# Two-level seven-product multiplication in the feed-forward up projections

## What is computed

```python
def swiglu(h, w_in, w_out):
    gt, up = jnp.split(h @ w_in, 2, axis=-1)
    return (jax.nn.silu(gt) * up) @ w_out
```

## Time and profile before

| | us |
|---|---|
| median of 3 runs | 3933.7 |
| the runs | 3933.52 to 3936.74 |
| span of the profiled execution | 3933.3 |

### The profile page before, as it was taken

One profiled execution on the slowest core, in us unless ns is written; L12 is line 12 of the kernel. 1 busy time (PEld: TensorE's weight loads), 2 busy tenths in 40 slices (PEclk: granted clock), 3 DMA queues, 4 the chain that ended last, 5 costly groups with the idle time before them and its releaser, 6 DMA issues.

```text
span 3933.3 us, 48502 instructions
## 1 busy us (share of the span) xinstructions
PE 3827.1 (97%) x18602; PEld 2867.3 (73%) x18602; DVE 2221.4 (56%) x3856; ACT 741.8 (19%) x1402; POOL 716.2 (18%) x570
## 2 busy tenths in 40 slices
PE   7999988999999999999999999999999999999998
PEld 3455567665555555688888877888789998778886
DVE  4255677354445313326564755654888888556546
ACT  2144455211110013421100000000311111100002
POOL 0048844000000000000000002120244343121200
PEclk9999999999999999999999999999999999999999
DMA  5244400222121121122322322232222222122321
GB/s 193 88 169 150 139 2 2 86 84 56 55 62 59 48 75 43 33 65 79 91 74 89 95 77 86 85 102 86 77 73 72 69 69 64 54 86 85 102 86 65
DMA packets 381407, 312.13 MB, mean 79 GB/s; under 512 B 9552, under 2 KB 349904, under 8 KB 381136
## 3 DMA queue, kind: packets, MB, share of 16 engines
q1 hardware_dynamic: 381264, 310.16, 25.3%
HBM read 308.03 MB, written 2.10 MB: 79 GB/s over the span
## 4 chain that ended last, share of the span: by engine, by line
PE 87%; POOL 5%; DVE 3%; ACT 2%; issue 1%; DMA 1%; POOLq 0%; SPq 0%; DVEq 0%; ACTq 0%
PE ps_lin L967 18%; PE ps_lin L867 10%; PE ps_d L967 9%; PE ps_lin L1741 6%; PE ps_d L867 5%; PE ps_c L967 4%; PE ps_lin L750 4%; PE ps_lin L767 3%; PE ps_d L750 3%; PE ps_lin L813 3%; PE ps_lin L1158 3%; PE ps_c L867 3%; POOL arena L3507 2%; PE ps_d L1530 2%; POOL arena L3504 2%; PE ps_c L750 2%
## 5 line engine op out<-in xcount | busy, mean ns | idle before, releaser
L3476 POOL TENSOR_TENSOR rstd<-square 128x512 f32<-128x512 f32 (+2 forms) x12 | 15.1, 1260 | 1542.5 <-ACT square L1919 1542.5
L967 PE MATMUL ps_lin<-arena,ring 128*128 128x256 f32 (+1 forms) x800 | 217.2, 424 | 1.1 <-DVE arena L2598 1.1
L867 PE MATMUL ps_lin<-arena,ring 128*128 128x256 f32 (+1 forms) x864 | 214.1, 401 | 0.0
L967 PEld LDWEIGHTS ps_lin<-arena,ring 128*128 128x128 f32 x800 | 151.8, 190 | 60.9 <-issue 2.9
L867 PEld LDWEIGHTS ps_lin<-arena,ring 128*128 128x128 f32 x864 | 164.2, 190 | 41.1
L967 PE MATMUL ps_lin<-hid_in,arena 128*128 128x256 f32 x832 | 188.6, 380 | 3.6 <-DVE arena L2625 3.6
L3479 POOL TENSOR_TENSOR rstd<-rstd,square 128x512 f32<-128x512 f32 (+2 forms) x58 | 75.5, 1301 | 630.9 <-ACT square L1919 630.0
L967 PE MATMUL ps_lin<-hid_in,mixed 128*128 128x384 f32 (+1 forms) x672 | 187.7, 432 | 0.0
L967 PE MATMUL ps_d<-arena,mixed 128*128 128x384 f32 (+1 forms) x672 | 187.7, 432 | 0.0
L2622 DVE TENSOR_TENSOR arena<-ring 128x1024 f32<-128x1024 f32 x84 | 102.9, 1225 | 146.3 <-PE ps_d L867 135.9
L967 PEld LDWEIGHTS ps_lin<-hid_in,arena 128*128 128x128 f32 x832 | 157.7, 190 | 27.7 <-DVE arena L2625 5.6
(11 more groups left out here) (546 smaller groups left out, 8101.4 us busy)
## 6 DMA issues: line engine op xcount, KB each, us to landing
ring<-in_ffn_w_in SPq DMA_DIRECT2D x88, 512.0 KB, 4.8
resid<-in_ada_w SPq DMA_DIRECT2D x20, 2048.0 KB, 7.9
ring<-in_mlp_w_up SPq DMA_DIRECT2D x64, 512.0 KB, 4.5
ring<-in_mlp_w_down SPq DMA_DIRECT2D x64, 512.0 KB, 4.4
ring<-in_attn_w_qkv SPq DMA_DIRECT2D x64, 512.0 KB, 4.8
ring<-in_ffn_w_out SPq DMA_DIRECT2D x32, 512.0 KB, 4.4
ring<-in_even_w_in SPq DMA_DIRECT2D x28, 512.0 KB, 5.0
ring<-in_sc_w_in SPq DMA_DIRECT2D x24, 512.0 KB, 4.6
```

Source lines behind the costliest of these rows:

```text
L867: last = mm(prod[i - 1], lhs[:, j, :], rhs(p), start=(g == j == 0), stop=(g == G - 1 and j == np_ - 1))
L967: last = mm(out, lhs[:, j, :], rhs[:, j, :], start=(j == 0), stop=(j == 3))
```

## The change

Both up projections work in 11 rounds of 256 gate and 256 up columns. The outer level cuts rows of the contraction in halves (H tiles 0 to 3 and 4 to 7), columns in gate and up, and tokens in halves, and has seven outer products in the order 1, 2, 7, 4, 5, 6, 3. Each outer product has 512 rows of contraction, 256 columns and half the tokens. It is done whole (two tiles, "a" and "b", of four matmuls of half the tokens) or is split once more in seven products of two matmuls of a quarter of the tokens: 192 columns in up0, 128 in up1. Outer product 4 is always whole, and in the first round only 1 and 2 are split: 62 of 77 are. The scheme is one in which the sums build on each other: inside a split product 1, 6, 7 and 4 accumulate in the same PSUM bank, and ScalarE copies its state out after 1, 6 and 7 ("partial") and 4 ("last_block"); 3 accumulates on 5.

GpSimd makes the four outer weight sums of a round (`outer_sums`), 1024 elements each, in the places of the loaded blocks. VectorE makes the four inner weight sums of a split product (`halves`, 256 elements each), the three blocks that are sums (`block_of`: "11", "22" and "12", a quarter of the tokens each, out of PSUM and a partial), the eight outer sums of a round (`outer_adds`, two tiles of half the tokens each), the products with the gate, and the inner sums of the inputs (`inner_inputs`, four each for six input blocks) and the outer ones T1 to T4. Partials and held products lie where constants were and in the norm's places. A round's four loads of 512 KB are issued as their places come free. Some semaphores are shared between loads. Product 3 of a split one and 4 come in TensorE's program after the next one's first products.

The diff's core:

```diff
+TWO_WIDTH, ROUNDS, OUTER = {"up0": T, "up1": LAT}, KF // 2, (1, 2, 7, 4, 5, 6, 3)
+OUTERS = 7 * ROUNDS
+INNER_SUMS = (1, 3, 2, 4)
+def outer(n):
+    return OUTER[n % 7]
+def split(n):
+    return 0 <= n < OUTERS and outer(n) != 4 and (n >= 7 or outer(n) < 3)
...
+SPLIT_LATER = {5: "T3", 6: "T1", 7: "T2", 8: "B22"}
+BLOCK_OF = {1: "B11", 2: "B21", 3: "B22", 4: "T4", 5: "T1", 6: "T2", 7: "T3"}
...
+    m["RAW2"] = {(1, 1): cut(ring, 0, 4, 2 * P), (1, 2): cut(ring, 1024, 4, 2 * P),
+                 (2, 1): cut(ring, 2048, 4, 2 * P), (2, 2): cut(ring, 3072, 4, 2 * P)}
+    m["SUM2"] = cut(big, 18944, 4, 2 * P)
+    m["OUT2"] = {1: m["RAW2"][1, 1], 2: m["RAW2"][1, 2], 3: m["RAW2"][2, 2], 4: m["RAW2"][2, 2],
+                 5: m["RAW2"][2, 1], 6: m["SUM2"], 7: m["SUM2"]}
...
+                for r in (1, 2):
+                    half_done(prev)(r - 1)
+                    for c in (1, 2):
+                        fill(0, r, c)
+                for i in range(1, ROUNDS):
+                    n = 7 * (i - 1)
+                    sp.wait_ge(s.two_sums, 4 * two_round(st, n) + 3)
+                    fill(i, 1, 1)
+                    if split(n + 4):
+                        sp.wait_ge(s.two_added, ADDED[st, n + 4, "half", 4])
+                    sp.wait_ge(s.two_made, MADE[st, n + 4, 4 if split(n + 4) else "b"])
+                    fill(i, 2, 1)
+                    sp.wait_ge(s.two_sums, 4 * two_round(st, n) + 4)
+                    fill(i, 1, 2)
+                    if split(n + 6):
+                        sp.wait_ge(s.two_added, ADDED[st, n + 6, "half", 4])
+                    sp.wait_ge(s.two_made, MADE[st, n + 6, 4 if split(n + 6) else "b"])
+                    fill(i, 2, 2)
...
+                def whole(n, t):
+                    b, w = mats[BLOCK_OF[outer(n)]], m["OUT2"][outer(n)]
+                    out = m["BANK2"][n % 2]["ab".index(t)][:, 0:hw]
+                    if t == "a":
+                        weights_there(n)
+                        if n < 7 and outer(n) == 3:
+                            pe.wait_ge(s.h_new, H_COUNT[late])
+                        elif n < 7:
+                            pe.wait_ge(s.two_added, ADDED[st, BLOCK_OF[outer(n)], 0])
+                        pe.wait_ge(s.two_taken, TAKEN[st, n - 2, 4 if split(n - 2) else "a"])
+                    elif split(n - 2):
+                        pe.wait_ge(s.two_added, ADDED[st, n - 2, 11])
+                    else:
+                        pe.wait_ge(s.two_taken, TAKEN[st, n - 2, "b"])
...
+                    c = slice("ab".index(t) * P, "ab".index(t) * P + P)
+                    steps(out, [(w[:, j, c], b[:, j, :]) for j in range(4)]).then_inc(s.two_made, 1)
...
+                def seventh(n, j):
+                    b, t = quarters(mats[BLOCK_OF[outer(n)]]), inner[BLOCK_OF[outer(n)]]
+                    w, ws = quarters(m["OUT2"][outer(n)]), m["HALF2"][n % 2]
+                    lhs, rhs = {1: (w[0], b[0]), 2: (w[2], b[2]), 3: (ws[4], b[3]), 4: (w[3], t[4]), 5: (ws[1], t[1]),
+                                6: (ws[2], t[2]), 7: (ws[3], t[3])}[j]
+                    chain_, second, fifth = m["BANK2"][n % 2]
+                    out = (second if j == 2 else fifth if j in (5, 3) else chain_)[:, 0:q]
+                    early = BLOCK_OF[outer(n)]
+                    if j == 1:
+                        weights_there(n)
+                        if n < 2:
+                            pe.wait_ge(s.h_new, H_COUNT[of] - KD + 4 * n + 2)
+                        else:
+                            pe.wait_ge(s.two_taken, TAKEN[st, n - 2, 4 if split(n - 2) else "a"])
+                    if j == 2:
+                        if n < 2:
+                            pe.wait_ge(s.h_new, H_COUNT[of] - KD + 4 * n + 4)
+                        elif split(n - 2):
+                            pe.wait_ge(s.two_added, ADDED[st, n - 2, 11])
+                        else:
+                            pe.wait_ge(s.two_taken, TAKEN[st, n - 2, "b"])
+                    if j == 5:
+                        pe.wait_ge(s.two_added, ADDED[st, n, "half", 1])
+                        if n == 0:
+                            pe.wait_ge(buf_free[1], BUFS[st])
+                        if split_before(n) is not None:
+                            pe.wait_ge(s.two_added, ADDED[st, split_before(n), 12])
+                    if j == 6:
+                        pe.wait_ge(s.two_taken, TAKEN[st, n, 1])
+                        pe.wait_ge(s.two_added, ADDED[st, n, "half", 2])
+                    if j == 7:
+                        pe.wait_ge(s.two_taken, TAKEN[st, n, 2])
+                        pe.wait_ge(s.two_added, ADDED[st, n, "half", 3])
+                    if j == 4:
+                        pe.wait_ge(s.two_taken, TAKEN[st, n, 3])
+                    if j == 3:
+                        pe.wait_ge(s.two_added, ADDED[st, n, 22])
+                        pe.wait_ge(s.two_added, ADDED[st, n, "half", 4])
+                    if j > 3 and n < 14:
+                        pe.wait_ge(s.two_added, ADDED[st, early, {4: 4, 5: 1, 6: 2, 7: 3}[j]])
+                    for k in range(2):
+                        last = mm(out, lhs[:, k, :], rhs[:, k, :], start=(k == 0 and j in (1, 2, 5)), stop=(k == 1),
+                                  skip_group_check=(j in (6, 7, 4, 3)))
+                    last.then_inc(s.two_made, 1)
+                pe.wait_ge(buf_free[0], BUFS[st])
+                for n in range(OUTERS):
+                    if split(n):
+                        seventh(n, 1)
+                        seventh(n, 2)
+                    else:
+                        whole(n, "a")
+                    if n == 0:
+                        square_sum(late, None)
+                    if split(n - 1):
+                        seventh(n - 1, 4)
+                    if split(n):
+                        seventh(n, 6)
+                        seventh(n, 5)
+                    else:
+                        whole(n, "b")
+                    if split(n - 1):
+                        seventh(n - 1, 3)
+                    if split(n):
+                        seventh(n, 7)
+                seventh(OUTERS - 1, 4)
+                seventh(OUTERS - 1, 3)
+                pe.wait_ge(s.two_taken, TAKEN[st, OUTERS - 1, 4])
+                pe.wait_ge(s.two_added, ADDED[st, OUTERS - 1, 12])
...
+            def two_level(st):
+                for n in range(OUTERS):
+                    if split(n) and n:
+                        partial(st, n, 1)
+                    elif not split(n):
+                        whole_block(st, n, "a")
+                    if split(n - 1):
+                        last_block(st, n - 1)
+                    if split(n) and n:
+                        partial(st, n, 2)
+                        partial(st, n, 3)
+                    elif not split(n):
+                        whole_block(st, n, "b")
+                    if n % 7 == 0 and n:
+                        gates(st, n // 7 - 1)
+                last_block(st, OUTERS - 1)
+                gates(st, ROUNDS - 1)
...
+            def halves(st, n, which):
...
+                    if k == 1:
+                        last = tt(w[1], a21, a22, add)
+                    elif k == 3:
+                        last = tt(w[3], a11, a21, sub)
+                    elif k == 2:
+                        last = tt(w[2], w[1], a11, sub)
+                        last = tt(w[4], a12, w[2], sub)
...
+            def two_level(st, late, following):
+                mats = m["TWO"][st]["mats"]
+                width = TWO_WIDTH[st]
+                b12 = mats["T3"]
+                for n in range(OUTERS):
+                    if split(n - 1):
+                        block_of(st, n - 1, 22)
+                    if split(n) and n:
+                        block_of(st, n, 11)
+                    if n == 1:
+                        dve.wait_ge(s.h_new, H_COUNT[late] - KD + 4)
+                        tt(mats["T1"], b12, mats["B11"], sub).then_inc(s.two_added, 1)
+                        dve.wait_ge(s.h_new, H_COUNT[late])
+                        tt(mats["T3"], mats["B22"], b12, sub).then_inc(s.two_added, 1)
+                    if n == 2:
+                        dve.wait_ge(s.two_added, ADDED[st, "T1", 0])
+                        tt(mats["T2"], mats["B22"], mats["T1"], sub).then_inc(s.two_added, 1)
+                    if n > 1 and split(n + 1):
+                        halves(st, n + 1, (1, 3, 2))
+                    if split(n - 1):
+                        block_of(st, n - 1, 12)
+                    if n == 2:
+                        dve.wait_ge(s.two_added, ADDED[st, "T2", 0])
+                        tt(mats["T4"], mats["B21"], mats["T2"], sub).then_inc(s.two_added, 1)
+                    if n > 1 and split(n + 1):
+                        halves(st, n + 1, (4,))
+                    if n % 7 != 1 and n % 7 != 3 and n:
+                        outer_adds(st, n - 1)
+                    if n % 7 == 1 and n > 1:
```

(53 more changed lines are left out.)

411 lines of the change are left out of this document (283 added, 128 removed).

## The result

The changed kernel takes 4002.9 us (median of 4 runs, 3998.8 to 4007.5), the one before 3933.6; the ratio is 1.0176, 95% interval 1.0162 to 1.019. I had predicted 3975, with a range of 3888 to 4012, and slower.

A forecast was written before the change was run, and what follows sets the result against it. VectorE's order with GpSimd's holds was taken to bound the changed kernel, TensorE the one before. up0 398.7 us against 398.8, up1 310.4 against 268.9, 41.5 longer: span 3933.3 becomes 3974.7, so 3975 us, range 3888 to 4012.

The forecast's parts named there:

- my own case: Whole kernel: VectorE's order with GpSimd's holds sets the pace, around 3975 us, own range 3945 to 3998; chance 0.50.
- The bound: Later rounds: VectorE with GpSimd's holds delays TensorE; period 27.5 us in up1 (24.2 before), 34.9 in up0 (36.1).
- the walk: One up1 round followed step by step: TensorE's 22.3 us plus stalls of 2.5 (block 22), 1.6, 0.85 and 0.25.
- rival 1: Both up projections: TensorE stays the bound, VectorE's lateness is absorbed; 42.7 us less, 3891 us; chance 0.22.
- rival 4: Both up projections: GpSimd sums met twice, or loads later; periods 36.5 and 30 us, total 4016; chance 0.15.
- GpSimd's holds: VectorE sums with two SBUF inputs wait for a whole GpSimd sum: 0 to 9.5 us a round; PSUM reads unheld.
- rival 2: VectorE's order binds, but GpSimd's sums fall where VectorE idles or reads PSUM: periods 33.9 and 24.1, 3929 us; chance 0.13.
- TensorE's work: TensorE's products in a later round: 32.5 us in up0, 22.3 in up1; 57 us less over both stages.
- Round 0: First round of each up projection: work, squares and waits for input sums, 41.5 us in up0, 29.5 in up1.
- The tails: End of each up projection: down projection's first weight sums delay the last block, 4.2 us in up0, 2.9 in up1.
- At 0: Loads, shared semaphores and GpSimd's squares behind the outer sums: costed at 0; uncovered, some us once.
- Round 1: Second round of each stage: 16 sums for later inputs come while VectorE is behind, 4 us in up0, 3 in up1.

The follow-up runs named there:

- experiment 1: Changed kernel with GpSimd's outer sums cut to one eighth after the first round, part of the computation left out: 3954.4 us, ratio 1.0052.
- experiment 2: Changed kernel with GpSimd sums begun later: a round's first and second, and in each stage's first round the first and third: 3995.8 us, ratio 1.0156.
- Experiment 7: Changed kernel with stage ends reordered: first-round GpSimd sums later, T4 behind T2, inner inputs and down projection's first weight sums a step earlier: 3984.8 us, ratio 1.0134.
- experiments 4: Changed kernel with VectorE itself making the first and second GpSimd sums of each later round: 3970.1 us, ratio 1.0089.
- 11: Kernel of 9, but VectorE itself makes the first and second GpSimd sums of each later round: 3942.8 us, ratio 1.0027.
- 9: Changed kernel, edits of 5, 6 and Experiment 7, but first GpSimd sum behind product 2's half-sums, one outer sum moved, silus awaiting the third: 3963.2 us.
- experiment 3: Changed kernel with all outer products whole in up1 from the second round on, the very last excepted: 3961.0 us, ratio 1.0066.
- 5: Changed kernel with later rounds' first GpSimd sum behind product 1's last half-sum, the second behind block 22 of product 2: 4024.3 us, ratio 1.0227.
- 6: Changed kernel with the last two of VectorE's four outer sums behind product 6 moved a step later: 4060.5 us, ratio 1.0322.

## Why the prediction was right, and where not

The direction and the mechanism came as forecast. The size came out too small: the change costs 67.3 us of the span where I had 41.4, and 4003 lies inside the stated range but above the 3945 to 3998 that I gave my own case. Of the 25.9 us missing 15.5 are the two rounds 0, 4.6 the two tails, 5.1 the first down products.

**The bound.** Right. up1's period was given as 27.5 and is 27.7, up0's 34.9 and is 34.9 to 35.1. The wait that ends last is where it was put:

```profile
PE ps_lin L1214 <- DVE rstd L2917: 8.6, 4, 2.4
PE ps_d L1214 <- DVE rstd L2917: 6.5, 3, 2.4
PE ps_lin L1214 <- DVE arena L2890: 2.9, 3, 1.0
PE ps_lin L1214 <- ACT rstd L2135: 1.8, 5, 0.4
```

Those are TensorE's waits from 1867 to 2060 us, seven rounds (total, times, longest): 2.2 us a round at block 22, for which the walk gave 2.5, then the half-sum, 0.4 a round against 1.2. So rival 1 (VectorE's lateness absorbed) falls, and rival 4 with its 30 us a round too. One sign that I had named failed: VectorE was to be over 90% busy in up1, and is 87% busy in a steady stretch (24.3 of 28 us).

**GpSimd's holds.** Right, and measured apart by experiment 1: the periods without them, worked out as 33.9 and 24.1 for rival 2, are 34.0 and 24.1. The Trainium skill (GPSIMD Engine Reference, section "1. Specifications") speaks of contention for VectorE instructions with two SBUF inputs; the rows say what it is here: the whole remaining length of the GpSimd instruction, 2.57 us for 0.41, or, where VectorE had begun, the reverse (experiment 2). Rival 2's condition (the sums fall in idle time) was wrong for S7, S5 and S3 and right for S6.

**TensorE's work** was 0.7 us a round too small: 23.0 and 33.1 us busy in experiment 1, against 22.3 and 32.5. In a round of up1 there six spacings, at the heads of four of the products, are 195 to 214 ns instead of 112, which the dense row of 96 didn't have. My stalls were about as much too large, and the two errors hide each other in the period: that 27.5 is so near 27.7 is in part luck. 192 columns at 163 ns was right: four take 0.65 us from start to start.

**Where TensorE's time went.** I had stalls only; the trace has two parts. In the same stretch TensorE is slow behind some of the stalls, and not behind others of the same length. Two windows of 28 us, one of each kind, and the four matmuls behind a stall of each kind:

```profile
1846.00:1874.00 28.00, 25.47 (x188) 24.13 (x188) 24.33 (x54) 8.35 (x28) 9.64 (x4) 0.94 0.25 80
1929.00:1957.00 28.00, 24.39 (x188) 22.70 (x188) 24.38 (x54) 8.25 (x28) 9.92 (x4) 1.00 0.26 77
```

```profile
1882.42 1.23 PE L1214 MATMUL ps_lin<-hid_in,arena 128*128 128x128 f32 x4 [2.04 <-DVE rstd L2917]
...
1937.96 0.71 PE L1214 MATMUL ps_lin<-hid_in,arena 128*128 128x128 f32 x4 [2.04 <-DVE rstd L2917]
```

The granted clock is 0.94 and 1.00, TensorE busy for 25.5 and 24.4 us with 188 instructions each, and the period is 27.7 to 27.8 both times. While VectorE sets the pace the slow clock costs nothing. It does cost where TensorE is the bound: 2.4 and 2.7 us in the first down products (granted clock 0.70 from 1205 to 1213 us, 0.57 from 2105 to 2112), and in round 0. The prediction had no term for it.

**Round 0, the step that failed most** (49.7 for 41.5, 36.8 for 29.5). I walked the deadlines of T3 and T4 there but not GpSimd's sums, which start as soon as the first loads land:

```profile
800.53 7.43 DVE L2827 SCALAR_TENSOR_TENSOR hid_in<-resid,small,rstd 128x256 f32<-128x256 f32 x8 [0.87 <-ACT rstd L2216]
800.87 2.35 POOL L4036 TENSOR_TENSOR arena<-ring 128x1024 f32<-128x1024 f32 x1 [5.47 <-DMA ring<-in_ffn_w_in]
803.18 2.52 POOL L4038 TENSOR_TENSOR ring<-ring 128x1024 f32<-128x1024 f32 x1
...
807.19 1.65 PE L1214 MATMUL ps_lin<-mixed,ring 128*128 128x192 f32 x4 [4.21 <-ACT const L2116]
...
821.05 3.14 DVE L2984 TENSOR_TENSOR mixed<-hid_in,mixed 128x1536 f32<-128x1536 f32 x1
...
824.29 4.45 PE L901 MATMUL ps_lin<-mixed,ring 128*128 128x384 f32 x8 [3.55 <-issue]
```

The scaling takes 7.43 us where it took 3.26; a block stands behind it, TensorE idles 4.21 us and then runs slowly (1.65 us for 0.81). T4 is held by S6 (3.14 for 1.75) and TensorE idles 3.55. Experiment 2 moves S7 and S6 alone, and round 0 of up0 falls to 44.1; what TensorE then waits for T3 and T4 is 1.99 and 2.16 us, near the 2.2 and 2.3 of my walk, so the walk of the deadlines was sound and the sums (and the slow clock behind the stalls) were what it lacked. In up1 it only falls to 35.5, since S5 there holds the making of T3 (3.35 us for 1.21). Experiment 7 moves S5 and T4 as well and gets 41.7 and 29.9; of these two edits the share of each isn't measured.

**The tails** were 6.0 and 5.7 us for 4.2 and 2.9. I had counted one idle stretch, at block 12 behind the weight sums (2.33 and 2.47 us in the trace). A second stands at block 22 behind the four outer sums (2.52 and 1.78): a stretch of the ordinary round, but no product of a next round fills it. Experiment 7 only moved time from the one to the other.

**At 0 and right, as far as is seen:** the shared semaphores (the loads landed in 3.8 us and none of TensorE's long waits in the two stages ends on one) and the squares (all that lies outside the stages and the first down products is 0.8 us). **Round 1:** the late inner inputs cost 2.7 and 3.4 us for 4 and 3.

## What to carry to other kernels

Scheme levels trade TensorE's work for VectorE's: count both per round, with every hold by the engine that shares the SBUF path, and add the second level only where TensorE's smaller sum stays the larger (here 33 us against 26 in up0; in up1 23 against 26 with GpSimd, 25 with VectorE). Work given to GpSimd isn't free for VectorE: where the helper's instruction is 2.35 us and VectorE's own 1.21, doing it oneself was 33 us faster with a better place for the first sum, and 20 with the orders mended (experiments 4, and 11 against 9). Where VectorE is idle half the time, as in experiment 3, GpSimd's sums cost nothing. When a sum, a wait or an order is moved, write down what stands behind it on its engine and who waits for it on the others; experiments 2, 5 and 6 missed on that question.
